# Exponentials of a routed block between u slices, and the residual of the third block two steps on, in a diffusion step with product-key experts

## What is computed

```
x = x + gt1 * (mix @ w_out)
h2 = _rmsnorm(x, n2) * (1 + sc2) + sh2
x = x + gt2 * _peer(h2, peer_wq, peer_subkeys, peer_u, peer_v)

def _peer(h, wq, subkeys, u, v):            # 8 heads, 128 keys per half, top 16 of 128 x 128 experts
    q = (hf @ wq).reshape(n, PEER_HEADS, 2, PEER_QUERY_DIM // 2)
    s = jnp.einsum('nhpd,hpkd->nhpk', q, subkeys)
    sv, si = lax.top_k(s, PEER_TOPK)
    ...                                     # best 16 sums of a first and a second half
    gates = jax.nn.softmax(top_v, axis=-1)
    act = gelu(einsum('td,tkd->tk', xb, u[eb]))
    return einsum('tk,tkd->td', gb * act, v[eb])
```

## Time and profile before

| | us |
|---|---|
| median of 3 runs (lowest, highest) | 3838.21 (3837.56, 3846.12) |
| the profiled execution | 3839.85 |
| its span from first to last instruction | 3838.0 |
| TensorE busy | 3654.0 (95%) |
| VectorE busy | 2597.6 (68%) |
| GpSimd busy | 1635.7 (43%) |
| ScalarE busy | 699.3 (18%) |

### The profile page before, as it was taken

The page is one execution under the profiler, slowest core; times in us unless marked ns, Lnnn a source line. Parts: engine busy times, 40 slices in busy tenths (PEclk is TensorE's granted clock), DMA queues, the critical chain, the costliest instruction groups (busy, mean ns, idle before and its releaser), DMA issues. The chain is left out here.

```text
span 3838.0 us, 39960 instructions
## 1 busy us (share of the span) xinstructions
PE 3654.0 (95%) x13726; PEld 2084.1 (54%) x13726; DVE 2597.6 (68%) x6024; ACT 699.3 (18%) x1575; POOL 1635.7 (43%) x1498
## 2 busy tenths in 40 slices
PE   5888989999999999999989899899999999999997
PEld 3456776655555555554455567665555555555543
DVE  7784879977667667677624748899777555565444
ACT  1152366300000000000013425661000000000000
POOL 0210155466566544444402003554877564444330
PEclk9989999999999999999999999999999999999999
DMA  6323045799999999999830122558999999899774
GB/s 270 104 90 116 19 141 149 253 368 389 381 369 377 379 376 371 376 375 361 347 125 2 68 105 73 148 152 299 407 410 410 379 346 368 341 357 356 293 299 156
DMA packets 365049, 1026.96 MB, mean 268 GB/s; under 512 B 30352, under 2 KB 132016, under 8 KB 364208
## 3 DMA queue, kind: packets, MB, share of 16 engines
q0 software_dynamic: 147456, 536.94, 36.5%
q1 hardware_dynamic: 118352, 436.07, 29.7%
q10 hardware_dynamic: 99040, 51.40, 4.9%
HBM read 965.07 MB, written 59.22 MB: 267 GB/s over the span
## 5 line engine op out<-in xcount | busy, mean ns | idle before, releaser
L1860 PE MATMUL ps<-colsT,arena 128*128 128x384 f32 x4096 | 1370.1, 489 | 4.3 <-DMA arena<-in_peer_ut 4.3
L1860 PEld LDWEIGHTS ps<-colsT,arena 128*128 128x128 f32 x4096 | 780.6, 191 | 585.9 <-issue 104.1
L1896 PE MATMUL ps<-arena 128*128 128x512 f32 x1536 | 676.5, 592 | 0.0
L1388 POOL DMA_INDIRECT proj<-in_peer_u,eidx x336 | 476.5, 1418 | 240.3 <-DVE modbc L1573 106.0
L1388 POOL DMA_INDIRECT proj<-in_peer_v,eidx x335 | 359.9, 1074 | 316.4 <-DVE colsT L1584 217.2
L1896 PEld LDWEIGHTS ps<-arena 128*128 128x128 f32 x1536 | 291.8, 190 | 345.2 <-issue 317.6
L1374 POOL TENSOR_SCALAR x<-iota,modbc 128x128 f32<-128x128 f32 x192 | 145.3, 772 | 692.2 <-ACT modbc L1699 550.2
L1573 DVE CUSTOM_DVE_ANT_0 proj<-proj,rows 128x1024 f32<-128x1024 f32 x336 | 399.6, 1223 | 57.7 <-DMA proj<-in_peer_u,eidx 55.7
L1584 DVE SCALAR_TENSOR_TENSOR colsT<-proj,modbc,colsT 128x1024 f32<-128x1024 f32 x330 | 409.6, 1286 | 14.2 <-DMA proj<-in_peer_v,eidx 14.1
L1388 POOL DMA_INDIRECT modbc<-in_peer_v,eidx x177 | 200.4, 1132 | 325.8 <-DVE colsT L1584 259.7
L1896 PE MATMUL ps<-arena,rows 128*128 128x512 f32 x768 | 337.8, 592 | 0.0
(11 more groups left out here) (293 smaller groups left out, 3736.8 us busy)
## 6 DMA issues: line engine op xcount, KB each, us to landing
arena<-in_peer_ut SPq DMA_DIRECT2D x256, 512.0 KB, 6.8
arena<-in_peer_v SPq DMA_DIRECT2D x256, 512.0 KB, 6.7
gmat_d<-arena ACTq DMA_DIRECT2D x24, 2048.0 KB, 10.1
arena<-gmat_d SPq DMA_DIRECT2D x64, 768.0 KB, 9.0
proj<-in_w_adaT SPq DMA_DIRECT2D x51, 512.0 KB, 9.3
modbc<-in_w_adaT SPq DMA_DIRECT2D x19, 512.0 KB, 9.0
rows<-in_w_adaT SPq DMA_DIRECT2D x18, 512.0 KB, 3.5
arena<-in_w_in SPq DMA_DIRECT2D x2, 4224.0 KB, 16.3
```

The source lines that it names most:

```text
L1388: pool.indirect_dma_start(ring[slots[at]], None, tab, bass.IndirectOffsetOnAxis(ap=eidx[:, b * SLOTS + q:b * SLOTS + q + 1], axis=0)).then ...
L1860: mm = pe.matmul(ps[:, 2 + j % 2, 0:ND], utab[:, j % UR, k], hT[:, k, NG:T], start=(k == 0), stop=(k == KT - 1))
L1896: mm = pe.matmul(ps[:, Y_BANKS[2 * d + c2], :], wT[j % CR][:, d * P:(d + 1) * P], vtab[:, j % VR, c2 * 512:(c2 + 1) * 512], start=(j == 0) ...
```

## The change

Four edits, in both layers:

- residual(2), mean(2) and normed(2) stand behind steps 3, 4 and 5 of route(0), no longer behind 1, 2 and 3.
- residual(4) stands after the first scatter of round 1, mean(4) and normed(4) after step 0 of route(1). Before, all three stood ahead of round 1. ScalarE's square(4) moves behind turned_rows(3).
- TensorE does the second half of out_proj(4) after turn(0). turn_rows(3), query(5) and turn_rows(4) come after place step 0; the query products 6 to 9 stand behind place steps 1 to 4, no longer 0 to 3.
- G_U: each round has three u slices behind place step 7, no longer two. Round 1 gives the one behind step 4 for it (that behind step 5 stays), round 2 the one behind step 3, round 3 the one behind step 6. exps(k) stands after the first gelu of step 7 and no longer after the last.

```diff
-        G_U = {1: (4, 5, 7, 7), 2: (-1, 1, 2, 3, 4, 5, 7, 7), 3: (-1, 1, 2, 3, 4, 5, 6, 7, 7)}
+        G_U = {1: (5, 7, 7, 7), 2: (-1, 1, 2, 4, 5, 7, 7, 7), 3: (-1, 1, 2, 3, 4, 5, 7, 7, 7)}
...
                 for step in range(STEPS):
                     route(0, step)
-                    if step == 1:
+                    if step == 3:
                         residual(2)
-                    if step == 2:
+                    if step == 4:
                         mean(2)
-                    if step == 3:
+                    if step == 5:
                         normed(2)
...
                 normed(3)
-                residual(4)
-                mean(4)
-                normed(4)
                 for k in range(1, HEAD_K + 1):
                     for step in range(STEPS):
                         if step < G_STEPS:
                             scatter_rows(k - 1, step)
+                        if k == 1 and step == 0:
+                            residual(4)
                         route(k, step)
+                        if k == 1 and step == 0:
+                            mean(4)
+                            normed(4)
...
                 def filler_out(k, step):
                     if (k, step) == (1, -1):
                         query_out(4)
+                    elif (k, step) == (1, 0):
                         turned_rows(3)
+                        square(4)
                         query_out(5)
                         turned_rows(4)
-                    elif k == 1 and step < 4:
-                        query_out(6 + step)
+                    elif k == 1 and step < 5:
+                        query_out(5 + step)
...
                     turned_out(k - 1)
-                    if k == 1:
-                        square(4)
...
-                        for _ in range(G_U[k].count(step)):
+                        for i in range(G_U[k].count(step)):
                             gelu(j)
                             j += 1
-                    exps(k)
+                            if step == G_STEPS - 1 and i == 0:
+                                exps(k)
...
                 def filler(k, step):
                     if (k, step) == (1, -1):
+                        out_proj(4, (1,))
                         query(4)
+                    elif (k, step) == (1, 0):
                         turn_rows(3)
                         query(5)
                         turn_rows(4)
-                    elif k == 1 and step < 4:
-                        query(6 + step)
+                    elif k == 1 and step < 5:
+                        query(5 + step)
...
                 out_proj(3, (1,))
-                out_proj(4)
+                out_proj(4, (0,))
```

## The result

The changed kernel takes 3862.81 us in the median (3859.77 to 3866.18, 5 runs), the kernel before beside it 3840.77 (3837.56 to 3846.12): a ratio of 1.0055 (95% interval 1.0043 to 1.0066), 22 us slower. The forecast was 19 us slower, and the change moved the way and by about the size that was said. The span of the profiled execution is 3861.0 us, 23.0 longer than before.

A forecast was written before the change was run, and what follows sets the result against it. TensorE was taken as the bound: its streamed pass has no hole, so head losses shift everything behind. Terms summed to +10.3 us in the first layer, +8.7 in the second, together +19: 3857.2 us median, range 3846 to 3868.

The forecast's parts named there:

- The wait before turn(0): Head: TensorE, with only half of out_proj(4) ahead of turn(0), waits 6.3 us for gates, not 2.0: +4.3 us.
- before turn_rows(4): Round 1: TensorE waits 2.8 us for normed(4), place step 1 adds 0.5 us: together +3.3 us.
- The clock: Half-clock stretch after the wait before turn(0), +2.2 us (0 to 3.4); the one after turn(2)'s wait goes, -1.7.
- The 0.4 us for the first tile: Round 1: the first u slice comes one place step after the query product that releases its load: +0.4 us.
- the score copies: Round 2: ScalarE's score copies precede its copies of place step 4, so removing the slice moves the step 0.5 us only.
- the late mark: Round 2: GpSimd's last mark, 6.80 us against L1438 and VectorE's next product, not 2.79; its wait stays.
- the moved slice: Round 2: slice taken from step 3 wins 0.5 us there and costs its 5.2 us again behind step 7.
- Wait for the gelu: Round 3: exps(3) ahead of two gelus holds the fourth slice after step 7: 3.7 to 6.3 us, middle +5.0.
- the tile's wait: Behind round 3: the 1.9 us wait for a table tile shrinks as loads and gathers start earlier: -1.6 us.
- The marks do get clear: Rival: round 2's last mark ends before L1438 starts; -15 us over both layers, 3842 us; chance 0.15.
- The exponentials did come sooner: Denied by a rival: ScalarE's queue holds the exponentials, the 6.3 us a layer stay, 3870 us; chance 0.05.
- the waits before the turns can go with nothing in their place: Rival: waits before turn(1) and turn(2) go and nothing replaces them; -16 us, 3822 us; chance 0.08.

The follow-up runs named there:

- the whole projection: The changed kernel with out_proj(4) whole ahead of turn(0) and no half of it behind: 3847.84 us, ratio 1.0022 to the kernel before.
- The run with the slices back: The changed kernel with the u slices of rounds 2 and 3 at their places of before: 3841.17 us, ratio 0.9994 to the kernel before.
- the run with exps(3) last: The changed kernel with exps(3) after the last gelu of round 3 again: 3861.75 us.
- the gap at step 5: The changed kernel with round 2's third slice taken from place step 5, not step 3: 3846.70 us, ratio 1.0017 to the kernel before.
- the run with the exponentials alone: The kernel before with exps(k) after the first gelu of place step 7, slices unmoved: 3822.2 us, ratio 0.9952.

## Why the prediction was right, and where it was off

**The start of a layer's stage: the waits stood where they were forecast.** VectorE was to wait 2.8 us before residual(3), and its timeline says so:

```profile
427.86 1.22 DVE L1404 TENSOR_TENSOR rows<-ps,modbc 128x1024 f32<-128x1024 f32 x1 [2.90 <-PE ps L1807]
```

The wait before turn(0) was forecast at 6.3 us and is 6.42; before turn_rows(4) 2.8, and it is 2.21. The 0.5 us for VectorE's pace at place step 1 do not show: no wait stands there. That the first is a loss and could have been avoided is shown by the whole projection: -15 us.

**The clock: under-sized.** 2.2 us were taken for one wait of 6.3. In the changed kernel these stretches (its length, then TensorE's busy time; the clock is the third number from the end) stand against the earlier trace rows:

```profile
438.00:444.80 6.80, 3.78 (x7) 2.04 (x8) 5.33 (x19) 1.19 (x5) 0.23 (x1) 0.51 0.00 1
472.10:475.30 3.20, 3.20 (x17) 3.14 (x16) 3.20 (x15) 1.68 (x3) 0.00 (x0) 0.50 0.00 0
601.80:605.00 3.20, 3.20 (x10) 2.29 (x9) 3.16 (x12) 3.14 (x9) 1.89 (x3) 0.50 0.54 154
629.10:635.70 6.60, 5.84 (x15) 4.03 (x16) 6.39 (x9) 0.60 (x1) 0.70 (x2) 0.50 0.32 94
```

At 0.50 half of the busy time is lost. Behind turn(0) that is 1.9 us and behind the wait for turn_rows(4) another 1.6, which I had not charged: 3.5 and not 2.2. Yet the sum up to the end of round 1 came out near the forecast: turn(1) is 5.9 and 8.4 us later in the two layers, against a sum of 7.1 (4.3 + 3.3 + 0.4 + 2.2 - 3.1), since in the first layer the slices behind step 7 ran with less half clock (16.25 us for three, where two took 12.32 in the earlier trace rows). That the slow clock stopped earlier there was not forecast and is luck. The 0.4 us for the first tile were not spent.

**Round 2: the mechanism right, the term too small.** I forecast that the score copies would hold place step 4. ScalarE's timeline of the changed kernel:

```profile
595.67 1.28 ACT L1713 ACTIVATE modbc<-iota,modbc 128x128 f32<-128x128 f32 x4 [0.44 <-ACT arena L1725]
596.99 0.63 ACT L1715 ACTIVATE modbc<-modbc 128x512 f32<-128x512 f32 x1
597.52 1.92 ACT L1677 ACTIVATE modbc<-ps 128x1024 f32<-128x1024 f32 x2
599.61 1.08 ACT L1725 ACTIVATE arena<-ps 128x512 f32<-128x512 f32 x2 [0.17 <-ACT modbc L1677]
```

The copies of the score block (L1677) end at 599.4, the next copy out of PSUM begins at 599.61, and TensorE goes on at 600.35 after 3.44 us. Also right: no wait before turn(2), and the late mark stayed. But the term was +1.5 us and the round came out at +4.2 and +2.9. What was missing is the clock again. The wait of 3.44 us, longer than any in that round before, was followed by 3.2 us at 0.50, 1.6 us lost (601.8 to 605.0 above). Behind the late mark the first layer ran 5.84 busy us at half clock, 2.9 lost, where the kernel before lost 1.6:

```profile
624.90:628.20 3.30, 3.15 (x10) 2.55 (x11) 3.13 (x8) 0.60 (x1) 0.10 (x1) 0.50 0.02 5
```

1.6 + 1.3 is what the first layer had over the forecast, 2.7, to within 0.2; in the second the first of the two is there alone, for 1.4. I had charged bare pairs with their waits alone. The run with the slices back parts the term in two. From the kernel before to it, round 2 gets 3.3 us shorter, and -3.1 was forecast for the wait that goes; from it to the changed kernel it gets 7.5 and 6.2 longer, and +4.7 was forecast for the moved slice. The second is the one that was mis-sized.

**Round 3: close, and so are its terms.** From turn(2) to the first v slice -1.7 + 5.0 - 1.6 = +1.7 us was forecast, +0.1 in the second layer, and +2.6 and +0.7 were measured. Wait for the gelu: 2.01. ScalarE's timeline shows the hold as it was described, 8.24 us of idle ScalarE in front of the exponential, and two gelus behind it:

```profile
721.24 1.28 ACT L1685 ACT_TABLE_LOAD   x1
730.77 0.31 ACT L1685 ACTIVATE proj<-proj 128x128 f32<-128x128 f32 x1 [8.24 <-DVEq L1463]
731.10 1.28 ACT L1691 ACT_TABLE_LOAD   x1
732.39 0.87 ACT L1691 ACTIVATE rows<-ps 128x384 f32<-128x384 f32 x2
```

The drain of some 1.4 us, which the Trainium skill ("ScalarE: Activation LUTs", What ACT_TABLE_LOAD costs) puts beside the table load, is not in these rows: the exponential ends at 731.08, the load follows at 731.10, and the gelu 0.01 us after it. VectorE's pace showed itself as 1.92 us of wait at place step 7; and the tile's wait fell from 1.9 to 0.85, not to 0.3. That the two waits trade against one another is what the run with exps(3) last shows. The run with the slices back shows that the terms were each about right: from the kernel before to it, this stretch gets 2.8 and 5.0 us shorter, against -1.7 - 1.6 and 1.6 more in the second layer; from it to the changed kernel it gets 5.4 and 5.7 longer, against +5.0.

**The rivals.** The marks do get clear of VectorE's products with the gap at step 5 (that run) but not with the change. The exponentials did come sooner. And the waits before the turns can go with nothing in their place, 19 us for one edit: the run with the exponentials alone reached this rival's 3822 us. It fell for the change only because the change carried two losses besides. As medians: the early exponentials are worth -19 us (3841 to 3822); the head and round 1 as changed cost +19 on top of them (3822 to 3841, the run with the slices back); the moved slices of rounds 2 and 3 cost +22 (3841 to 3863). That comes to +22. By the ratios, each to its own runs of the kernel before, the three are -18, +16 and +23.

**Slips of the working.** The second layer follows 1881 us behind the first (turn(0) at 445.56 and 2326.19), not 1981. The terms of round 2 add up to +1.6 and not +1.5, and 469.2 to 471.9 is 2.7 us and not 2.8. None of them moves the forecast.

## What to carry to other kernels

When an engine waits for a value, first look at what stands between the value and its use on the engine that makes it; moving the exponential ahead of one gelu in ScalarE's order was worth 19 us alone, and the slice moved along as extra cover paid for something that two slices covered already. Work taken out from between two steps costs nothing only if no other engine used that time: here ScalarE's marks and copies lived in it, and in round 2 the stretch that was laid bare was the one with the score copies in it. And work that is moved behind a wait, as the half projection was, is cover given away: ask whether the value will be there when the engine is.

## What the runs showed of the hardware

- A wait of TensorE had a price beyond its own length. 3.44 us were followed by 3.2 us at a clock of 0.50 with TensorE busy throughout (1.6 us lost), 6.42 us by 3.78 busy us at 0.51 (1.9 lost), and even the 2.21 us before turn_rows(4) by 3.2 busy us at 0.50. It did not follow each time. Behind the 3.15 us before turn(1), the kernel before ran its next slice in 5.33 us, which is full speed; its timeline of TensorE:

```profile
555.08 5.33 PE L1860 MATMUL ps<-colsT,arena 128*128 128x384 f32 x16
```

- GpSimd's four mark operations take 2.8 us alone and 6.6 to 6.8 us against two VectorE products, each over two SBUF operands. Keeping them apart by a wait on VectorE was worth 8 us of 3842, although the wait lies on the path to the gates.
